# Side-input projection of block 1: one output tile per attention turn, its norm inside ffn1

## What is computed

```python
h = _rms_norm(x, in_norm_g[l])
y = h @ w_in[l] + b_in[l]            # gates, mLSTM, HGRN2, and q, k, v of a banded attention
...
s_out = swa_sink_attention(q_s, k_s, _heads(sv, SWA_KV_HEADS), swa_sinks[l])
x = x + jnp.concatenate([m_out, h_out, s_out], axis=-1) @ w_out[l]
u = _rms_norm(x, mlp_norm_g[l]) @ w_up[l]
x = x + jnp.square(jax.nn.relu(u)) @ w_down[l]
gate = jax.nn.sigmoid(_rms_norm(x, ple_norm_g[l]) @ w_ple_gate[l])
e = _rms_norm(p[l] @ w_ple_proj[l], ple_post_norm_g[l])
x = x + gate * e
```

## Time and profile before

| | |
|---|---|
| median of 3 runs | 3099.55 us (3099.26 to 3101.38) |
| profiled execution | 3100.26 us, span from first to last instruction 3098.1 us |
| busy TensorE / its weight loads | 3035.8 us (98%) / 2421.5 us (78%) |
| busy VectorE / ScalarE / GpSimd | 57% / 40% / 10% |
| mean granted TensorE clock | 0.995 of full |
| transfers | 259 MB, 84 GB/s over the span |

### The profile page before, as it was taken

How to read it: one execution, slowest core, us unless ns; L and a number is a source line. 1 busy time by engine, 2 the same in 40 slices (tenths; PEclk the granted TensorE clock), 3 DMA queues, 4 the chain that set the end, 5 groups by cost and what they waited for, 6 DMA issues and landing times.

```text
span 3098.1 us, 38472 instructions
## 1 busy us (share of the span) xinstructions
PE 3035.8 (98%) x15228; PEld 2421.5 (78%) x15228; DVE 1761.0 (57%) x2584; ACT 1254.3 (40%) x2084; POOL 299.8 (10%) x257
## 2 busy tenths in 40 slices
PE   7999999999999999999999999999999999999998
PEld 5777888887777888887667878888866678788886
DVE  7755644457666544467775635344577755354444
ACT  6644322245554322344444534232344444342322
POOL 2011100011011100011001102000110011020001
PEclk9999999999999999999999999999999999999999
DMA  3111233322112233332112322333211133223332
GB/s 139 55 49 57 94 99 99 95 96 82 56 48 67 94 99 99 95 95 74 55 55 89 123 68 82 96 98 100 89 60 57 48 96 113 64 89 97 101 95 82
DMA packets 73726, 259.14 MB, mean 84 GB/s; under 512 B 8020, under 2 KB 10200, under 8 KB 73176
## 3 DMA queue, kind: packets, MB, share of 16 engines
q1 hardware_dynamic: 72824, 252.99, 25.8%
q0 software_dynamic: 736, 3.87, 0.4%
HBM read 254.73 MB, written 2.10 MB: 83 GB/s over the span
## 4 chain that ended last, share of the span: by engine, by line
PE 83%; issue 6%; DVE 6%; POOLq 1%; ACT 1%; DVEq 1%; DMA 0%; POOL 0%; ACTq 0%
PE bank L569 68%; PE bank L499 2%; PE bank L1127 1%; POOLq L3072 1%; DVE w_lo L2183 1%; PE bank L793 1%; PE bank L1138 1%; PE bank L1352 1%; PE bank L1331 1%; PE bank L1082 1%; PE bank L1148 1%; PE bank L1152 1%; PE bank L823 0%; DVE der L2789 0%; PE bank L877 0%
## 5 line engine op out<-in xcount | busy, mean ns | idle before, releaser
L569 PE MATMUL bank<-a_hi,w_hi 128*128 128x512 f32 x2120 | 848.2, 400 | 20.3 <-DVE w_lo L2183 15.7
L569 PE MATMUL bank<-a_hi,w_lo 128*128 128x512 f32 x2120 | 828.7, 391 | 0.0
L569 PE MATMUL bank<-a_lo,w_hi 128*128 128x512 f32 x2120 | 827.9, 391 | 0.0
L2183 DVE TENSOR_TENSOR w_lo<-w_raw,w_hi 128x1024 fp32r<-128x1024 f32 (+1 forms) x474 | 611.2, 1290 | 285.5 <-ACT w_hi L1458 283.8
L1458 ACT ACTIVATE w_hi<-w_raw 128x1024 fp32r<-128x1024 f32 (+1 forms) x474 | 494.9, 1045 | 416.2 <-DMA w_raw<-weights 415.7
L569 PE MATMUL bank<-b_hi,w_hi 128*128 128x512 f32 (+1 forms) x1516 | 572.0, 377 | 2.0 <-DVE w_lo L2183 0.9
L569 PE MATMUL bank<-b_lo,w_hi 128*128 128x512 f32 (+1 forms) x1516 | 564.0, 372 | 0.0
L569 PE MATMUL bank<-b_hi,w_lo 128*128 128x512 f32 (+1 forms) x1516 | 564.0, 372 | 0.0
L569 PEld LDWEIGHTS bank<-a_hi,w_hi 128*128 128x128 f32 x2120 | 399.7, 189 | 121.9 <-issue 22.4
L569 PEld LDWEIGHTS bank<-a_hi,w_lo 128*128 128x128 f32 x2120 | 399.5, 188 | 85.3
L569 PEld LDWEIGHTS bank<-a_lo,w_hi 128*128 128x128 f32 x2120 | 400.2, 189 | 83.0 <-issue 3.3
(11 more groups left out here) (340 smaller groups left out, 3170.4 us busy)
## 6 DMA issues: line engine op xcount, KB each, us to landing
w_raw<-weights SPq DMA_DIRECT2D x458, 512.0 KB, 3.5
w_raw<-weights SPq DMA_DIRECT2D x16, 384.0 KB, 3.0
x<-x SPq DMA_DIRECT2D x8, 256.0 KB, 7.1
mem<-mem POOLq DMA_DIRECT2D x2, 1024.0 KB, 5.2
out<-x SPq DMA_DIRECT2D x8, 256.0 KB, 2.1
mem<-mem SPq DMA_DIRECT2D x1, 1024.0 KB, 12.0
ple<-ple POOLq DMA_DIRECT2D x2, 512.0 KB, 4.0
o<-c_level SPq DMA_DIRECT2D x1, 512.0 KB
```

What stands on the lines that cost most here:

```text
L569: last = mm(bank[unit_bank(u) if at is None else at][:, 0:cols], w[:, u % SLOTS, ks], t[:, k, 0:cols], start=(k == begun and n == 0), stop ...
L2183: tt(w_lo[:, u % SLOTS, w], w_raw[:, u % SLOTS, w], f32(w_hi[:, u % SLOTS, w]), ALU.subtract).then_inc(w_lo_ready, 1)
```

## The change

The eight output tiles of the side projection are summed one per turn in turns 2 to 7 and two in turn 12, in banks 7 (tiles 0 to 5 and 7) and 6 (tile 6), instead of in a stage of their own. `proj` is gone. Its two weight units stand in the stream before the output projection's. VectorE copies a tile in the turn in which it is made. The dummies of turns 2 to 7 and 12 are gone. p is loaded earlier (GpSimd's queue, after the norm sums of q and k) and lies in tiles of y that are free then; ScalarE rounds p_hi before the turns, VectorE makes p_lo in turns 0 and 1. VectorE splits the units 25 and 26 of the layer in turns 8 and 10. In ffn1 the sum over x's squares is issued in the middle of the third unit, r_x follows it, the squares of e are taken in the eight up steps, their sum is issued in the middle of the second down unit, and the scaling of e follows in the down steps. In the gate the two sets of y tiles change places.

```diff
 def stream():
-        order += [(at + j, 8) for j in range(WIN_T + 8)]
+        order += [(at + j, 8) for j in range(WIN_T)]
         order += [(at + WIN_T + 72, 0), (at + WIN_T + 76, 0)]
+        order += [(at + WIN_T + j, 8) for j in range(8)]
...
                 def window_outputs(m):
+                    pe.wait_ge(e_taken, 8 * l + 6 + 2 * m)
...
+                def side_tile(i):
+                    u, j = c.unit, i % 4
+                    if j == 0:
+                        pe.wait_ge(w_lo_ready, u + 1)
+                    if i == 0:
+                        pe.wait_ge(p_ready, 2 * (l + 1))
+                        pe.wait_ge(h_out, 2 * l + 1)
+                    elif i < 6:
+                        pe.wait_ge(e_taken, 8 * l + i)
+                    else:
+                        pe.wait_ge(a_took, 4 * l + 2)
+                    for k in range(2):
+                        ks = slice((2 * j + k) * P, (2 * j + k + 1) * P)
+                        for n, (w, t) in enumerate(((w_hi, p_hi), (w_hi, p_lo), (w_lo, p_hi))):
+                            last = mm(bank[6 if i == 6 else 7][:, :], w[:, u % SLOTS, ks], t[:, k, :],
+                                      start=(k == 0 and n == 0), stop=(k == 1 and n == 2))
+                    last.then_inc(e_made if j < 3 else unit_done, 1)
+                    if j == 3:
+                        c.unit += 1
...
                 for s in range(16):
-                    if s in (2, 3, 4, 5, 6, 7, 11, 12):
+                    if s == 11:
                         pe.wait_ge(a_copied, 16 * l + s - 1)
-                        if s == 11:
-                            pe.wait_ge(a_kept, 4 * l + 2)
+                        pe.wait_ge(a_kept, 4 * l + 2)
                         kept_busy(4 + s % 2, 1, P)
                     if s + 2 < 16:
                         window_scores(s + 2)
                     window_turn(s)
+                    if 2 <= s < 8:
+                        side_tile(s - 2)
+                    if s == 12:
+                        side_tile(6)
+                        side_tile(7)
...
                 def chunk(first=False):
                     if first:
-                        pe.wait_ge(e_taken, 8 * l + 4)
                         pair(a, a_ready)
-                        pe.wait_ge(e_taken, 8 * (l + 1))
-                        unit(a)
-                        sum_squares()
+                        unit(a, midway=sum_squares)
                     for j in range(3 if first else 0, 8):
                         unit(a)
                     for j in range(8):
-                        unit(h, ready=h_ready if j == 0 else None)
+                        unit(h, ready=h_ready if j == 0 else None, midway=sum_squares if first and j == 1 else None)
...
# ScalarE, ffn1
                             f(h[0][:, j, :], y[:, 16 + j % 2, :], ACT.Square).then_inc(h_hi_ready, 1)
+                            if first:
+                                square(y[:, j, :])
 
                         step(hidden)
-                        if first and j == 2:
-                            root_of_mean()
...
                 ahead(c.unit + 3)
+                root_of_mean()
+                act.wait_ge(e_taken, 8 * (l + 1))
                 chunk(first=True)
...
# VectorE, mix1
+                def side_take(i):
+                    if i == 0:
+                        dve.wait_ge(h_summed, 2 * (l + 1))
+                    if i == 5:
+                        dve.wait_ge(g_nsum, 3 * (l + 1))
+                    if i % 4 < 3:
+                        dve.wait_ge(e_made, 6 * l + 3 * (i // 4) + i % 4 + 1)
+                    else:
+                        dve.wait_ge(unit_done, c.unit + 1)
+                    dve.tensor_copy(y[:, i, :], bank[6 if i == 6 else 7][:, :]).then_inc(e_taken, 1)
...
                     if s < 2:
                         rope_add(3 + s)
+                        side_low(s)
+                    if 2 <= s < 8:
+                        side_take(s - 2)
+                    if s == 12:
+                        side_take(6)
+                        side_take(7)
+                    if s in (8, 10):
+                        ahead(first + 25 + s // 10)
...
# VectorE, ffn1
                 ahead(c.unit + 3)
+                recip(r_x)
                 chunk(first=True)
...
# GpSimd, mix1 (was in out1, behind a wait for the attention's outputs)
+                pool.wait_ge(g_nsum, 3 * l + 2)
+                pool.dma_start(ple[:, :, :], dram["ple"][l].rearrange("p (a b) -> p a b", a=2)).then_inc(ple_landed, 16)
```

More of the change, by code:

```diff
@@ L1061, in ffn1 @@
                 chunk()
[L1063 to L1072, removed]
-                            b = unit_bank(base + j)
-                        elif j < 3:
-                            b = 5 + j
-                        else:
-                            pe.wait_ge(e_taken, 8 * l + 1)
-                            b = unit_bank(base)
-                        for k in range(2):
-                            ks = slice((2 * j + k) * P, (2 * j + k + 1) * P)
-                            for i, (w, t) in enumerate(((w_hi, p_hi), (w_hi, p_lo), (w_lo, p_hi))):
-                                last = mm(bank[b][:, :], w[:, u % SLOTS, ks], t[:, k, :],
-                                          start=(k == 0 and i == 0), stop=(k == 1 and i == 2))
-                        last.then_inc(e_made if j < 3 else unit_done, 1)
-                    c.unit += 1
-                    if part == 0:
-                        sum_squares()
             def gate(l):
@@ L1786, in mix1 @@
                 finish(22)
+                act.wait_ge(ple_landed, 16 * (l + 1))
+                for k in range(2):
+                    f(p_hi[:, k, :], ple[:, k, :], ACT.Copy).then_inc(p_hi_ready, 1)
                 ahead(first + 26)
@@ L1815, in mix1 @@
                 f(g_r[:, 56:72], g_r[:, 56:72], ACT.Sqrt, bias=eps, scale=1.0 / 64).then_inc(g_root, 1)
-                c.unit += WIN_T
+                ahead(first + WIN_T + 4)
+                c.unit += WIN_T + 2
             def round_o(h, k):
@@ L2156, in _ @@
                 out1(l)
-                proj(l)
                 ffn1(l)
@@ L2580, in mix1 @@
                 window_recips(1)
-                ahead(first + 25)
                 recips(2, 56, 16)
@@ L2604, in out1 @@
                     lo_h(h, k, o[:, k, :])
-                for k in range(2):
-                    dve.wait_ge(p_hi_ready, c.count(p_hi_ready))
-                    tt(p_lo[:, k, :], ple[:, k, :], f32(p_hi[:, k, :]), ALU.subtract).then_inc(p_ready, 1)
+                ahead(c.unit + 3)
                 for k in range(8):
                     step(add_to_x(k, (a, col("mlp_g", l, k))))
-            def proj(l):
-                base = c.unit
-                ahead(base + 3)
-                for part in range(2):
-                    for j in range(4):
-                        if j < 3:
-                            dve.wait_ge(e_made, c.count(e_made))
-                        else:
-                            dve.wait_ge(unit_done, c.unit + 1)
-                        b = 5 + j if part == 1 and j < 3 else unit_bank(base + j if part == 0 else base)
-                        dve.tensor_copy(y[:, 8 + 4 * part + j, :], bank[b][:, :]).then_inc(e_taken, 1)
-                    dve.drain().then_inc(bank_free, 1)
-                    c.unit += 1
-                    ahead(c.unit + 3)
-                recip(r_x)
             def ffn1(l):
```

62 lines of the change are left out of this document (29 added, 33 removed).

## The result

The changed kernel takes **3111.55 us** (median of 6 runs, 3110.33 to 3112.73) against 3100.11 us for the kernel before in the same rounds (6 runs, 3096.83 to 3101.38). The ratio is 1.0038, with a 95% interval of 1.0028 to 1.0048: slower by about 0.4%. The forecast was 3104.8 and the range ended at 3110.0, so the direction holds and the size doesn't; the rival that came nearest, a colder TensorE, was put at 3108.0. What follows explains the profiled execution of the changed kernel: 3110.36 us, span 3108.4.

A forecast was written before the change was run, and what follows sets the result against it. TensorE, busy 98% of the span, was taken as the bound. Per layer -10.9 + 7.0 + 3.0 + 3.5 = +2.6 us, +5.2 for two layers, gave 3104.8 us, range 3097.5 to 3110.

The forecast's parts named there:

- a colder TensorE: Rival: fewer dummies and new holes slow TensorE's clock once a layer, 3108.0 us; chance 0.18 together with waits at upper bounds.
- The old stage: Removing the projection's own stage, 48 matmuls of 0.227 us, gains 10.9 us a layer; its 0.90 us sum moves to ffn1.
- Turns 8 to 13: Attention's later turns: a late copy, a wait for VectorE's products and two side tiles add 3.0 us a layer.
- The wait in ffn1: TensorE waits for w_lo at ffn1's fifth unit, adding 3.5 us a layer, bounds 2.5 to 4.6.
- The partial collision with GpSimd: In ffn1, GpSimd's additions overlap VectorE's chain to w_lo, adding 0.2 us; a full collision would be 1.05.
- the waits' upper bounds together: Slower case: the added waits all at their upper bounds; shares the chance of 0.18 with the colder clock.
- The sign that I had named: Granted clock below 1.00 in the attention turns would show the forecast wrong on the slow side.
- a hole of 1.56 us ahead of 218.72: Argument against the colder clock: this hole in the old trace left the clock at 1.00 in the turns behind it.
- a gain of 1.9 us: Credit in turns 2 to 7 for removing six dummies: 2.3 us of them, of which 1.9 us count.
- Turns 2 to 7: Six side tiles in the banded attention, less credits and plus new waits, add 7.0 us a layer, bounds 5.5 to 9.
- the wait for p_lo: TensorE waits 1.1 us at the first side tile until VectorE has made both halves of p_lo.
- The single credits inside: Deductions in turns 2 to 7: 1.9 us for dummies, 0.9 for waits and small gaps, 0.3 for groups starting during drains.

The follow-up runs named there:

- e1: Changed kernel with the sum over x's squares issued after the sixth block of ffn1's first pair instead of in the third unit: 3100.76 us, ratio 1.0004 to the kernel before.
- e3: Changed kernel with both p_lo subtractions on VectorE moved ahead of turn 0: 3109.16 us, ratio 1.0034 to the kernel before.
- e6: Changed kernel with 8 dummy products (16 matmuls of 256 columns) ahead of ffn1's fifth unit: 3108.02 us, ratio 1.0025 to the kernel before.
- e7: Changed kernel with e1's sum placement, the first p_lo split ahead of turn 0 and the second in turn 0: 3095.3 us, ratio 0.9983 to the kernel before.
- e2: Changed kernel with the dummies of turns 2 to 7 and 12 put back: 3111.04 us, ratio 1.004 to the kernel before.
- e5: Kernel before the change, with only its dummies of turns 2 to 7 left out: 3103.37 us, ratio 1.0007 to the kernel before.
- e4: Changed kernel with 14 dummy products of 256 columns (28 matmuls) ahead of ffn1's fifth unit: 3113.32 us, ratio 1.005 to the kernel before.
- e8: e7 with side tile 6 waiting for one product instead of both, and turn 10's w_lo split moved behind turn 12's maxima: 3094.24 us, ratio 0.9982 to the kernel before.

## Why the prediction was wrong

**The frame held.** TensorE sets the time, the two layers run alike, and the sum by stretches is the right sum: with the clock's share of 3.1 us taken out of a layer's 6.17 it gives 3.1, against 2.6 foretold. The old stage gave 10.8 us back (11.69 less the 0.90 of the sum that moved; 10.9 predicted). Turns 8 to 13 cost 2.88 (3.0). The wait in ffn1 is 3.5 as worked out from the chain of root, reciprocal, evictions, squares and split (TensorE went on 26.3 us after the pair began, 26.2 foretold), and e1 shows that the whole of it comes from the sum's place in the third unit: this was the best-founded term and the one that could be repaired. The partial collision with GpSimd, put at 0.2, was right too: the split at ffn1's fifth unit took 1.45 us, not 1.23 and not 2.28. The rule of the Trainium skill ("GPSIMD Engine Reference", Specifications), that VectorE instructions with two SBUF inputs contend with GpSimd, agrees with it and with e3's splits, 1.37 us against 0.69.

**The step that failed**: the forecast's sum has no term for TensorE's clock behind the waits that it adds. It put that at nothing, on the strength of one hole that had done no harm, and kept "A colder TensorE" as a rival with 0.18 for itself and the waits' upper bounds together. The rival's mechanism was right and its price was near: I put 1.6 us on a spell, and e6 measures 1.58 (once, in e3, it was 2.6). Its number of spells was wrong. I allowed one a layer, in the turns; there are two, and the second stands behind the 3.5 us wait that the forecast itself had put into ffn1. I priced that wait as time lost and never asked what it does to the clock. The first spell can be read off the two layers of e1, 29.82 and 28.32, and off the starts: from the first side tile to the second are 4.11 us in the changed kernel and 2.60 in e7. Both give 1.5 us. Two spells of 1.5 and 1.6 in two layers are 6.2 us, of a miss of 6.75. The sign that I had named for this, a clock below 1.00 in the turns, is there: the mean granted clock of 217 to 247 us is 0.94 in the changed kernel and 1.00 before.

**The evidence against it was read too widely.** I argued that a hole of 1.56 us ahead of 218.72 had left the clock at 1.00. That hole stands ahead of 2.3 us and more of level sums without a break. The hole at 228.54 in the changed kernel is shorter, 0.98, but comes some 1.1 us after another of 0.60, with only light scores and transposes between. e2 shows that with 0.38 for the first of these and a dummy there, the same 0.99 does no harm. In e3 a single hole of 1.41 there did no harm either. So the longest hole alone doesn't decide; in the turns every layer that fell has two holes close together with light work between them, and so have some layers that didn't fall. That this is what matters is a reading of the traces and was not tested by itself, and how much of either it takes isn't settled here. The dummies whose removal I booked as a gain of 1.9 us were what stood between. Where the Trainium skill ("TensorE: Matmul & The Clock Gate", Part 1) has the throttled state as the default and activity as what releases it, e5 and e2 agree with it, and I should have given it more than its share of 0.18.

**Turns 2 to 7**, 7.0 predicted: 8.72 measured, of which 1.5 is the clock, so 7.2 otherwise (28.32 - 21.09 in e1's layer 1). Without the wait for p_lo I had 5.9, and e7 shows 27.10 - 21.09 = 6.01. The single credits inside are less good than their sum: by e5 the dummies are worth 0.5 in time, not 1.9, as the waits for exponentials of the earlier trace rows grow when they go, from 1.4 to 2.1 us in e5's layer 1. With side tiles in their place the exponentials have more time, and there the dummies cost 1.27 (e2).

**The fall is not the same in every run of the same order.** With the hole of 0.98 at the first side tile and no dummies, six layers of other kernels were traced besides the two of the changed one: e1 falls in layer 0 and not in layer 1, e4 the other way round, e6 in layer 0 only. That is five of eight. Behind the unfilled wait of 3.5 us it falls in four of six (e2 in layer 1, e3 in layer 0, the changed kernel in both). Where neither the hole nor the wait is there, in e7 and e8, none of the four layers falls at either place. One more stretch does so in all kernels, before too: the first projections of a layer, near 71, 151, 764 and 845 us, where the number of slow matmuls changes from kernel to kernel, up to 12 in a spell and, in the changed kernel near 845, none. That may be some of the 2 to 6 us by which the runs of one kernel scatter, and it limits what the last two edits of e8 can show.

**What stays open**: why one layer falls and the other doesn't; what sets the length of a spell (1.5 to 2.6 us lost in the changed kernels, 5.2 in e5); and whether the scatter of the medians hides half of e8's 2.2 us, or whether it is given back further on.

## What to carry to other kernels

A wait on the engine that bounds the kernel costs its length and then, often, a spell at half rate behind it, here mostly 1.6 us on top of 3.5; book both, for each wait that a change opens, and look at the spacing of the matmuls behind a hole rather than at the mean clock (0.995 against 0.993 for 6 us). When a stage is dissolved, ask what it was covering: here the norm's root and the weights' split, and moving one sum of squares forward by 5.4 us in each layer was worth some 10.7. Dummies that look like pure cost may hold the clock through a thin stretch, so take them out alone first and measure.

## What the runs showed of the hardware that I had not expected

- Without its six dummies the kernel before ran its turns at a mean granted clock of 0.77 over 30 us in one layer and at 1.00 in the other, the same instructions in both.
- Filling a 3.5 us wait in each layer with 16 dummy matmuls, which end about when the wait does, made the program some 3 us faster (3111.55 to 3108.02 in the medians, 2 x 1.58 in the trace), though what TensorE waits for came no earlier.
- A split of 512 columns on VectorE took 1.37 us a piece under GpSimd's products and 0.69 clear of them; a single one beside them took 1.07 (e7).
